# One pass ordering in a fused two-layer hybrid decoder step: the fourth group's gate projections before the output chunks, and all engines' work lists rewritten

## What is computed

```python
def ssd_mixer(h, conv_buf, ssm_state, ...):
    proj = h @ w_in                     # z (2048), xBC (3072), dt (32 heads)
    xBC = silu(causal_dwconv(xBC, conv_buf, conv_w) + conv_b)      # 4 taps
    dt = softplus(dt + dt_bias); A = -exp(A_log)
    y, new_state = ssd_chunked(x, dt, A, B, C, ssm_state)          # chunks of 128 tokens
    y = (y + Dskip * x) * silu(z)
    y = grouped_rmsnorm(y, norm_w, 4)   # a mean square over each of 4 groups
    return y @ w_out, new_buf, new_state
```

## Time and profile before

| what | value |
|---|---|
| median of 3 runs | 935.51 us (932.94 to 937.43) |
| the profiled execution's own time | 931.63 us |
| its span, first to last instruction | 929.9 us |
| PE busy | 885.2 us (95%) |
| DVE busy | 626.9 us (67%) |
| ACT busy | 406.0 us (44%) |
| POOL busy | 143.7 us (15%) |

### The profile page before, as it was taken

The page is one execution under the profiler, slowest core; times in us unless marked ns, Lnnn a source line. Parts: engine busy times, 40 slices in busy tenths (PEclk is TensorE's granted clock), DMA queues, the critical chain, the costliest instruction groups (busy, mean ns, idle before and its releaser), DMA issues.

```text
span 929.9 us, 19386 instructions
## 1 busy us (share of the span) xinstructions
PE 885.2 (95%) x7385; PEld 871.4 (94%) x7385; DVE 626.9 (67%) x1039; ACT 406.0 (44%) x757; POOL 143.7 (15%) x95
## 2 busy tenths in 40 slices
PE   5999999999999999979999999999999999989996
PEld 4898888999989999978999999999999999979996
DVE  4589999889997999977475555555555555554543
ACT  6666667556763676735242222222222222243343
POOL 5303621333133413530000000000000000000000
PEclk9999999999999999999999999999999999989999
DMA  7337536563665437613243333333333333212212
GB/s 181 102 102 209 153 94 188 160 162 95 191 183 154 120 110 220 199 51 115 68 114 111 91 91 91 90 90 91 90 90 90 90 90 90 91 59 96 93 46 92
DMA packets 162992, 107.99 MB, mean 116 GB/s; under 512 B 5000, under 2 KB 155152, under 8 KB 162368
## 3 DMA queue, kind: packets, MB, share of 16 engines
q1 hardware_dynamic: 123876, 76.15, 28.1%
q10 hardware_dynamic: 38756, 30.61, 11.3%
q0 software_dynamic: 304, 0.48, 0.3%
HBM read 95.35 MB, written 12.14 MB: 116 GB/s over the span
## 4 chain that ended last, share of the span: by engine, by line
PE 53%; DVE 1%; ACT 1%; issue 1%; POOLq 0%; POOL 0%; DVEq 0%; ACTq 0%
PE bank L1790 20%; PE pair L1790 20%; PE pair L2055 5%; PE bank L2055 5%; PE pair L1850 3%; DVE ybuf L1682 0%; PE bank L1863 0%; POOLq L90 0%; ACT sqb L804 0%; ACT xT L963 0%; DVE sqs L1377 0%; ACT L493 0%; PE bank L2120 0%; DVE yr L1349 0%; POOL sqb L437 0%
## 5 line engine op out<-in xcount | busy, mean ns | idle before, releaser
L513 ACT ACTIVATE whi<-raw 128x1024 fp32r<-128x1024 f32 x136 | 143.5, 1058 | 343.7 <-PE bank L1790 139.2
L1790 PE MATMUL pair<-hhi,whi 128*128 128x260 f32 x1136 | 231.9, 285 | 0.3 <-DVE acc L1174 0.3
L1790 PE MATMUL pair<-hhi,wlo 128*128 128x260 f32 x1136 | 229.3, 283 | 0.0
L1790 PE MATMUL pair<-hlo,whi 128*128 128x260 f32 x1136 | 228.8, 283 | 0.0
L1044 DVE TENSOR_TENSOR wlo<-raw,whi 128x1024 fp32r<-128x1024 f32 x132 | 185.0, 1403 | 23.5 <-ACT whi L513 21.2
L1790 PEld LDWEIGHTS pair<-hhi,whi 128*128 128x128 f32 x1136 | 175.5, 189 | 2.4 <-DVE acc L1174 1.2
L1790 PEld LDWEIGHTS pair<-hlo,whi 128*128 128x128 f32 x1136 | 175.5, 189 | 0.0
L1790 PEld LDWEIGHTS pair<-hhi,wlo 128*128 128x128 f32 x1136 | 175.4, 189 | 0.0
L1790 PE MATMUL bank<-hhi,whi 128*128 128x260 f32 x512 | 103.1, 282 | 0.9 <-ACT sqs L498 0.9
L1790 PE MATMUL bank<-hhi,wlo 128*128 128x260 f32 x512 | 103.2, 283 | 0.0
L1790 PE MATMUL bank<-hlo,whi 128*128 128x260 f32 x512 | 103.0, 283 | 0.0
(11 more groups left out here) (242 smaller groups left out, 1305.9 us busy)
## 6 DMA issues: line engine op xcount, KB each, us to landing
raw<-in_sc_w_in SPq DMA_DIRECT2D x64, 512.0 KB, 4.0
raw<-in_ssd_w_in SPq DMA_DIRECT2D x40, 512.0 KB, 3.9
abc<-a_rows ACTq DMA_DIRECT2D x16, 512.0 KB, 4.3
sample<-in_state_ssm ACTq DMA_DIRECT2D x16, 512.0 KB, 7.1
out_new_ssm_s<-sample ACTq DMA_DIRECT2D x16, 512.0 KB, 4.2
raw<-in_ssd_w_out SPq DMA_DIRECT2D x16, 512.0 KB, 4.0
raw<-in_sc_w_out SPq DMA_DIRECT2D x16, 512.0 KB, 3.5
sample<-bc_rows ACTq DMA_DIRECT2D x4, 1024.0 KB, 6.7
```

The costliest lines, as they stand in the source:

```text
L513: act.activation(whi[:, slot, :], raw[:, slot % RAW, :], ACT.Copy).then_inc(hi_done, 1)
L1790: mm = pe.matmul(b, w[:, slot, k * P:(k + 1) * P], h[:, k, cols], start=(k == 0 and i == 0), stop=(k == KT - 1 and i == 2))
```

## The change

The arithmetic, the tiles, the weight chunks and their number stay as they are. LAST, the chunk order of the fourth pass, puts z0 to z3 right behind x3 and the four output chunks of the third group (now l0 to l3) behind them. The lists of PE, DVE, ACT and POOL are rewritten for all passes; the loops are cut at another place (before `within(g, 0)` and x3 on PE). Cut to its core:

```diff
-LAST = ["B", "C", "x0", "x1", "x2", "x3", "o0", "z0", "z1", "z2", "z3", "l1", "l2", "l3"]
+LAST = ["B", "C", "x0", "x1", "x2", "x3", "z0", "z1", "z2", "z3", "l0", "l1", "l2", "l3"]
```

ACT, from the first tap of x0 to the second step's segments (the old lines, then the new ones):

```diff
                 first_tap(g, 2)
-                norm_root(g - 1)
+                load_state(g, 0)
                 copy_turned(g)
+                split(g, "x0")
                 tanh_conv(g, 2)
-                split(g, "C")
                 decay_channels(g, 0)
+                decay(g, 0)
                 first_tap(g, 3)
-                y_high(g - 1, 0)
-                y_high(g - 1, 1)
+                norm_root(g - 1)
+                store_state(g - 1, 3)
+                load_state(g, 1)
                 load_abc(g, 1)
-                y_high(g - 1, 2)
-                y_high(g - 1, 3)
+                final_state(g - 1, 3)
                 tanh_conv(g, 3)
-                split(g, "x0")
                 store_bc(g)
                 first_tap(g, 4)
+                y_high(g - 1, 0)
                 split(g, "x1")
-                store_state(g - 1, 3)
+                y_high(g - 1, 1)
+                y_high(g - 1, 2)
                 load_bc(g)
-                load_state(g, 0)
+                y_high(g - 1, 3)
                 segments(g, 1)
-                load_state(g, 1)
                 decay(g, 1)
                 tanh_conv(g, 4)
```

More of the change, by code:

```diff
@@ L451, in _ @@
             for g in range(-1, GROUPS):
+                inject(g - 1, 2)
+                weigh(g - 1, 3)
                 read_out(g - 1, 2)
@@ L467, in _ @@
                 read_out(g, 1)
+                if g == -1:
+                    early_low()
                 add_squares(g, 0)
-                weigh(g, 3)
-                inject(g, 2)
+            inject(3, 2)
+            weigh(3, 3)
             read_out(3, 2)
@@ L903, in _ @@
-                decay(g, 2)
-                split(g, "z0")
-            tanh_z(3, 1)
+            final_state(3, 0)
+            store_state(3, 0)
+            decay_channels(3, 1)
+            load_abc(3, 2)
+            scale_state(3, 1)
+            load_state(3, 2)
+            tanh_conv(3, 5)
+            split(3, "z0")
+            segments(3, 2)
+            tanh_z(3, 1)
+            decay(3, 2)
+            decay_channels(3, 2)
+            load_abc(3, 3)
+            store_state(3, 1)
@@ L1396, in _ @@
[L1396 to L1406, removed]
+                silu_z(g - 1, 1)
+                silu(g - 1, 5)
+                residual0(g - 1, "o2", 0)
@@ new lines, in _ @@
+                conv(g, 0)
+                sample_add(g - 1, 3)
+                if g == 0:
+                    decays_to_end()
+                gate(g - 1, 2)
+                silu(g, 0)
+                next_low(g, "B")
+                weigh_earlier(g - 1, 3)
+                skip(g - 1, 3)
+                conv(g, 1)
+                sample_out(g - 1, 3)
+                if g == 0:
+                    by_channel()
+                add_earlier(g - 1, 3)
+                silu(g, 1)
+                gate(g - 1, 3)
@@ L1427, in _ @@
+                next_low(g, "C")
+                conv(g, 2)
+                silu(g, 2)
+                sample_x(g, 0)
+                next_low(g, "x0")
+                mask_cb(g)
+                weigh_dt(g, 0)
+                conv(g, 3)
+                causal(g, 0)
+                norm_scale(g - 1, 0)
+                norm_scale(g - 1, 1)
+                norm_scale(g - 1, 2)
+                silu(g, 3)
+                copy_bc(g)
+                norm_scale(g - 1, 3)
                 if g == -1:
@@ L1458, in _ @@
-                causal(g, 0)
-                if g == -1:
-                    dt_rest()
-                norm_scale(g - 1, 0)
-                silu(g, 2)
-                norm_scale(g - 1, 1)
-                next_low(g, "C")
-                norm_scale(g - 1, 2)
-                norm_scale(g - 1, 3)
-                copy_bc(g)
-                weigh_dt(g, 0)
-                conv(g, 3)
+                recur(g, 0)
+                weigh_dt(g, 1)
                 y_low(g - 1, 0)
                 y_low(g - 1, 1)
-                silu(g, 3)
@@ new lines, in _ @@
+                weigh_earlier(g, 0)
+                residual0(g, "o0", 1)
+                weigh_dt(g, 2)
+                recur(g, 1)
+                sample_x(g, 1)
+                next_low(g, "x2")
+                silu_z(g, 0)
+                add_earlier(g, 0)
+                next_low(g, "x3")
+                if g == -1:
+                    cache_taps()
+                sample_out(g, 0)
+                residual0(g, "o1", 0)
+                next_low(g, "o0")
+                gate(g, 0)
```

372 lines of the change are left out of this document (175 added, 197 removed).

## The result

The changed kernel takes 951.52 us (median of 4 runs, 949.64 to 954.32), the kernel before, beside it, 935.21 (932.94 to 937.43). The change makes it slower: the ratio is 1.0196, with a 95% interval of 1.0172 to 1.0219. Of the executions profiled, before took 931.63 us (span 929.9), after 949.64 (span 947.9): +18.0.

A forecast was written before the change was run, and what follows sets the result against it. PE was taken as the bound, changeable only in its idle time, with DVE binding the fourth pass's tail. Terms -1.5 + 6.0 + 5.8 + 5.8 + 0.1 = +16.2 gave 947.8, 951.7 at the median, put down as 951; eight in ten 938 to 962.

The forecast's parts named there:

- the sum of +16.2: All passes of layer 0 together: -1.5 + 6.0 + 5.8 + 5.8 + 0.1 us, taking the profiled execution to 947.8.
- Lead-in: From the preceding z3 to the conv of x3: ACT's load waits uncovered for its store; 6.6 us lost per pass.
- The wait before o0's second half, put at 2 to 4: Sign on PE in passes two to four: a wait of 2 to 4 us there would show the forecast right.
- The 5.8: Loss per pass, third and fourth: lead-in of 6.6 us, less about 0.85 because z3 ends earlier.
- The term of -0.85 per lead-in for the chunk states: On PE, chunk 3's states move behind z3, so z3 was to end about 0.85 us earlier.
- The second pass: Its lead-in starts from DVE, not z3: 6.6 us less what DVE's lag hides, taken as +6.0.
- The first pass: No store to wait for; part of a short wait covered and within(0, 2) no longer waiting: -1.5 us.
- The tail: Fourth pass's end: residual -0.6, collisions +2, l2's second half later, sum +1.9; less group-sum idle saves about 1.8; total +0.1.
- The claim that the order alone is neutral up to the group sums: Fourth pass: the new chunk order alone gives -0.6 us, since DVE's last gate decides when the group sums start.
- Rival (d): As the sum, but PE's clock drops after each 4 us wait, 1.8 each, and both collisions come: 959 to 966; 12%.
- The term of 1.9 us per lead-in: From silu of x1 to PE's next output half: DVE loses one inject to POOL's port lock; bounds 0 to 2.95.
- The landing time: In the lead-in, the store that ACT's load waits for lands 4.2 us after issue, the median; formula estimate 3.2.

The follow-up runs named there:

- e2: Changed kernel with the store of state 3 moved earlier on ACT, before squares, so it has landed when the load is reached: 942.4 us.
- e9: e6 with the chunk states of chunk 3 put back ahead of projection z3 on PE: 942.71 us.
- e12: Kernel before with only the chunk states of chunk 3 moved behind projection z3 on PE: 942.09 us.
- e5: Kernel before with the fourth pass's new chunk order alone, l0's low half on DVE right behind the last gate's low half: 936.28 us.
- e6: e2 with DVE's weigh and skip of the earlier sequence's last chunk put ahead of the silu of B: 939.44 us.
- e11: e9 with the conv of x3 moved on DVE ahead of causal and the low half of x1: 953.91 us.
- e3: Kernel before with the store of state 3 and load of state 1 put side by side on ACT behind x1's first tap: 933.33 us.
- e1: Changed kernel with the load of state 1 moved back behind the segments on ACT, away from the store: 945.1 us.

## Why the prediction was right, and where not

The time is right: 951 forecast, 951.52 measured, and +18.0 in the profiled executions against the sum of +16.2. That the median is hit within 1 us is in part luck: the sum is 1.8 us short, and the 3.9 us that I added for the median over the profiled execution turned out as 1.9. Its steps, one by one.

**Lead-in: place and kind right, sizes smaller.** ACT idle of 4.11 to 4.22 us behind the second root (about 4), DVE idle of 3.2 to 3.3 before the silu of x1 (about 4), PE waits of 3.28, 3.42, 3.44 before the turn of x1 (4 to 5), no wait before the group sums (shorter than 4.06): all at the places named. From the end of the first tap of x1 to its silu I had 340.1 to 350.3, 10.2 us; the changed kernel takes 9.1, 9.0 and 9.0, the kernel before 5.2 in each pass. So the silu loses 3.8 to 3.9 to this chain, not 5.1: the store goes out 0.7 us before the root ends and lands after 3.24 and not 4.2, while the three issues take 1.6 and not 1.2. The wait before o0's second half, put at 2 to 4, was 0.05, 1.15 and none. From that silu to o0's second half I had 16.7 us against 15.2; it is 16.1 and 15.7 in passes two and three, against 15.6 in both before. Both terms were too large. That the whole still comes out near 5.8 (+4.7 and +5.8 for the third and fourth pieces of the table) owes to things I had at nothing: waits of 1.23 and 0.99 us before z3, and the lower clock behind the wait in the lead-in of pass four.

**Lead-in: the reason is right for half of it only.** The 5.8 is meant as a silu 5.1 us later. Three of these make 15 us; with the wait taken away (e2), the whole kernel gains 9.1. The three passes are not alike: in e2 the fourth piece falls by 4.3 us, to within 1.5 of before, while the third doesn't (104.7). There PE waits 1.85 before o0's second half and then runs it at the lower clock (4.43 us for 24 matmuls instead of 3.1). DVE's lateness shows again at other places in e2: 2.90 us before the projection of x1 in pass two, 2.09 before the `within` of x1 and 3.65 before an output half in pass four.

**The term of -0.85 per lead-in for the chunk states: not shown.** PE's work is the same in both places. In the changed kernel the projection z3 follows o3's output halves directly and waits for the residual that frees its PSUM pair, 1.23 and 0.99 us in passes two and three. With the states back in front of it this wait is gone (e9), but the kernel isn't faster. In the lists of the kernel before z3 doesn't wait without them either; there the move costs 8 us by way of the recurrence (e12). I had counted it as a gain without asking who reads the states and what stands behind that reader.

**The second pass: mis-sized.** For the first and the second pass together I had -1.5 + 6.0 = +4.5; the table has 89.1 - 80.5 = +8.6. The first pass is right: from x3 to z3 it takes 33.8 us against 35.3, the -1.5 put down. So the lead-in of the second costs 10.1 and not 6.0. But between z3 and the next x3 PE waits twice where I had counted nothing:

```profile
117.82 0.51 PE L1799 MATMUL pair<-hhi,whi 128*128 128x260 f32 x2 [2.04 <-DVE zh L1374]
...
135.80 0.80 PE L1799 MATMUL pair<-hhi,whi 128*128 128x260 f32 x2 [2.21 <-DVE acc L1187]
```

The projections of C and x1 wait for DVE's silu of z3 and conv of C, and behind each wait PE runs at the lower clock. A window over the projection of C:

```profile
117.80:125.40 7.60, 7.58 (x50) 7.58 (x51) 7.42 (x13) 4.83 (x13) 3.46 (x2) 0.78 0.65 189
```

These 48 matmuls take 7.56 us, not 6.0, those of x1 7.42. So 2.04 + 2.21 + 1.6 + 1.4 = 7.3 us come from two places beside the one forecast, against waits of 0.62, 0.28 and 1.08 us in this stretch of the kernel before.

**The tail: mis-sized the other way.** Forecast +0.1, measured 96.8 - 99.3 = -2.5. Waits of 1.92 + 1.49 + 4.06 and the slow group sums have gone; 0.78, 0.57, 0.31, 1.95 and 1.17 stand in their place, and a projection of 7.54 us behind the 1.95. Against that gain I had put 2 us more of collisions and 0.5 for l2's second half, which with the residual's -0.6 made 1.9. l2 costs next to nothing: its halves wait 0.13 and 0.09. The claim that the order alone is neutral up to the group sums stands (e5).

**The clock: the rival's mechanism, without its size.** Rival (d) wanted 1.8 us after each wait of 4. After the 3.44 us wait the `within` takes 1.98 us instead of 1.1 and x3's projection 6.59, in all 1.4 to 1.5; pass two is the same, but after the 3.42 of pass three both run at full speed (1.09 and 6.02). Windows over the three, from the wait's end to about the end of x3's projection (columns as above, the clock third from the end):

```profile
155.50:164.70 9.20, 9.15 (x70) 8.60 (x71) 8.92 (x18) 8.15 (x19) 2.94 (x2) 0.81 0.36 140
260.10:268.50 8.40, 8.40 (x77) 8.06 (x78) 8.22 (x17) 7.58 (x18) 2.91 (x2) 1.00 0.42 153
363.70:372.80 9.10, 9.03 (x69) 8.46 (x70) 8.80 (x19) 7.99 (x19) 3.21 (x2) 0.81 0.38 138
```

So part of (d) happened, in two passes of three, and already at waits of 2. With the projections of C and x1 and the 7.54 of the tail, five places cost 1.4 to 1.6 us each, some 7.5 in all, where the kernel before pays 1.7 once, at its group sums. That is most of the 9 us that PE's busy time has grown by, and a third of the whole difference; my sum had only the 1.8 that were to be won.

**The port.** The exclusive lock from the Trainium skill (SBUF — State Buffer, section "SBUF: two separate sides") shows in e2's silu of B, 2.86 us against 0.69 while GpSimd's read_out runs, and its cure in e6. The term of 1.9 us per lead-in was too large. In the changed kernel the y_low beside `weigh` took 1.55 instead of 0.69 in each of the three lead-ins, +0.86 where I had allowed up to 1.05. The inject met the conv, which reads PSUM and took its usual 2.3 us for three taps. Nor is the loss all or nothing: the silu in the earlier trace rows ends 0.56 us behind the inject and lost 1.34 of the inject's 1.90, since it came 0.43 after its start.

**The landing time: the median was right, the store was not.** The median of the sixteen landings is 4.1 us in the page of after (4.2 in the earlier trace rows), but they spread from 3.2 to 7.8, and the three stores that ACT waits for landed after 3.24 and 3.25. The Trainium skill (DMA: Bandwidth & Descriptors, section "Anatomy of one DMA") gives an estimate of 3.2 by its formula, and these three agree with it. The page fits the formula to DMAs that GpSimd issues, while these go from ACT's queue, so the agreement is that of this trace alone.

So the forecast is right with errors that cancel: +4.1 in the piece from x3 to x3 of pass two, -1.1 and 0.0 in the next two, -2.6 in the tail, and +1.4 in the run-up and behind layer 0, together 1.8. What stays open is how the 7 us that are left in e6 are shared among the new orders of DVE, ACT and PE: the single edits, put back one on top of the other, made none faster (e9 to e11).

## What to carry to other kernels

Before a store and the load into the same buffer stand next to each other in one engine's queue, look what the consumer behind them has as slack: ACT's wait of 1.9 to 3.6 us cost nothing that the time shows in one order, one of 4.1 cost 2 to 3 us a pass in another. When an item moves on one engine, find its reader on every other engine and what is queued behind that reader; one microsecond of work behind a projection cost 8 us in two passes together. Orders that were searched together are not a sum of edits: test an edit in the lists in which it will stand.

## What the runs showed of the hardware

TensorE's granted clock fell to the lower level after waits much shorter than the 4.06 us of the earlier trace rows: the window over the projection of C stands at 0.78 after a wait of 2.04, and the 48 matmuls of a projection took 7.4 to 7.6 us. It is not a matter of the wait's length alone: after 1.92 us, in the earlier trace rows, the output half ran at full speed (3.11 us for 24 matmuls, 3.03 where nothing is waited for), and after 3.42 us, in pass three of the changed kernel, so did all that followed. Nor do the instructions around the wait decide. Passes two, three and four of the changed kernel have the same ones, and the clock fell in two of the three. Before o0's second half in pass two, the kernel before waited 2.35 us and ran at full speed (3.13 us), while e3, with the same list on PE, waited 1.91 and then took 4.64:

```profile
162.50:167.10 4.60, 4.53 (x25) 4.56 (x26) 4.00 (x6) 1.30 (x3) 1.13 (x1) 0.63 0.59 179
```

What decides, no run here separates. The price differs as much: the output half that waits for 3.7 us in pass four takes 5.41 us in e1 and 3.11 in e2, whose lists on PE are the same too.

This is a part of a wait's price: in e12 the waits of 3.93 and 3.92 us each brought 1.6 us of slower matmuls with them.
